# Strassen FFN in a two-layer decoder: order of weight loads, row sums and shared additions

## The chip, the cores and the metric
The kernel is one program on 1 core of a Trainium2 chip. The metric is the device time of one execution in microseconds (us); the median of 3 runs before the change is 2208.37 us (2204.72 to 2210.13). The engines are named as the profile names them: PE (TensorE, matmuls), DVE (VectorE), ACT (ScalarE), POOL (GpSimd) and SP (SyncE, which issues DMAs here).

## The reference
Two layers, each a token mixer and then a gated MLP with a causal convolution of width 3, on x of 1024 x 1024 in float32. The change touches the MLP alone (and, by two lines, the start of layer 1's mixer):

```python
def conv_ffn(x, norm_g, w_up, conv_w, conv_b, w_down):
    h = causal_depthwise_conv(rms_norm(x, norm_g) @ w_up, conv_w, conv_b)
    g, u = jnp.split(h, 2, axis=-1)
    return (jax.nn.silu(g) * u) @ w_down

for layer in range(DEPTH):
    x = x + (pool_diffattn_layer if layer % 2 == 0 else mlstm_layer)(x, ...)
    x = x + conv_ffn(x, ...)
```

w_up is 1024 x 5632, w_down 2816 x 1024. The hidden width is cut in FC = 22 rows of 128 channels.

## The kernel before
Each float32 matrix is cut into a high and a low part, and a product is three matmuls (high x high, high x low, low x high) of 128 x 128 weights with 512 columns.

**Up stage.** Block j (0 to 21) makes row j of g and of u at once, as one 2 x 2 Strassen-Winograd product: seven half-size products of 12 matmuls each, on PE in the order a11, s2, s3, s1, a22, a12, s4. Their weights come from two raw tiles (a g tile and a u tile, loaded by SP into a ring of 3): POOL makes the sums s1 to s4 (`pool_s1` to `pool_s4`), ACT copies each of the seven to its high part (`act_cut`, a "cut"), POOL subtracts to get the low part (`pool_low`, a "low"). The ring holds 6 of these weights, so a cut waits until PE has finished the product 6 places earlier. DVE adds the products up: u2, u3, then c22, c21 (hg, the g row) and c11, c12 (hu, the u row), multiplies both by the norm factor (`dve_hg`, `dve_hu`), and after ACT's centre tap (`act_center`, into PSUM) adds the two other taps. ACT's silu and DVE's `dve_gated` give the gated row in one of two buffers; SP stores it in `gated_rows`. PE's a22 of block j waits for u3 of block j; u2 and u3 stand on DVE behind the taps of hu of block j-1.

ACT's own order in block j is: cut a12(j), silu(j-1), the copy p1(j), cut s4(j), centre of hu(j-1), then cuts a11, s2, s3, s1, a22 of block j+1 and the centre of hg(j). Everything on an engine runs in program order.

**T sums.** Rows 4 to 19 are taken in pairs into a second Strassen product in the down stage. When both rows of a pair are stored, four sums of halves are made in place (`dve_pair_t`, on DVE in the even blocks 6 to 20) and stored by SP (`sp_pair_out`). The buffers are needed again by `dve_gated` two rows later.

**Down stage.** Rows 20, 0, 1, 2 are multiplied plainly (4 rows, `pe_down`), then come 8 Strassen blocks m = 0 to 7 (`pe_block`), then rows 3 and 21. In a Strassen block the order on PE is again a11, s2, s3, s1, a22, a12, s4, and the weights are made as above. Each block m also has to bring in the pair inputs for block m+2: ACT issues the loads (`act_pair_load`), cuts them in two parts (`act_pair_split`, half 0 and half 1), DVE makes the low parts (`dve_pair_low_half`). The sums on DVE are u1, u2 (a shared U), e22, c22, e21, a11, c12. U is shared: only in the last two blocks (m = 6, 7) is it added to three output quarters, v22, v21, v12. In block 6 DVE also makes the low parts of rows 3 and 21 (`dve_gated_low`), which wait for ACT's cuts of those rows (`act_gated_high`), and these stand on ACT behind the cut s3 of block 7. PE's a11 of block 7 waits for DVE's a11 addition of block 6, its a22 for e22, its s4 for c22.

**Start of layer 1.** The first three weight tiles of the mixer are cut by POOL (`pool_cut`); POOL also adds the squares of the norm (`add_squares`).

Of the kernel before, what the change touches and what calls it, by code (L numbers as in the profile page):

```python
# [10 lines left out]
ALU = mybir.AluOpType  # L11
# [18 lines left out]
DOWN_ORDER = (FC - 2, 0, 1, 2, 3, FC - 1)  # L30
# [53 lines left out]
def program(nc, x_in, pos_in, wall, pool_w, params, lam4, consts, scratch, gated_rows, out):  # L84
    with ExitStack() as ctx:
# [1448 lines left out]
        def block_parts(m):  # L1534

            shared = ("v22", "v21", "v12") if m >= N_BLOCK - 2 else ()
            return ("u1",) * (m >= 2) + ("u2",) + shared + ("e22", "c22", "e21", "a11", "c12")
# [392 lines left out]
        def dve_pair_t(dve, f, r):  # L1930

            b11, b12, b21, b22 = (f.ab[:, i, h * HALF:(h + 1) * HALF] for i in range(2) for h in range(2))
            at0 = f.l * SUMS + 3 * (KC // 2) + 4 * r
            dve.wait_ge(a_out, 16 * (f.l * A_OUT + out_at(PAIR0 + 2 * r + 1)))
            dve.tensor_tensor(b22, b22, b12, ALU.subtract).then_inc(tt_made, 1)
            dve.wait_ge(tt_made, at0 + 1)
            dve.tensor_tensor(b12, b12, b11, ALU.subtract).then_inc(tt_made, 1)
            dve.wait_ge(tt_made, at0 + 2)
            dve.tensor_tensor(b11, b11, b22, ALU.add).then_inc(tt_made, 1)
            dve.wait_ge(tt_made, at0 + 3)  # L1940
            dve.tensor_tensor(b21, b21, b11, ALU.subtract).then_inc(tt_made, 1)

# [9 lines left out]
        def dve_block_add(dve, f, m, name, to, room):  # L1952

            dve.tensor_tensor(to, room.rearrange("p (a s) -> p a s", a=2), to, ALU.add).then_inc(parts, 1)  # L1954

# [8 lines left out]
        def dve_block(dve, f, m):  # L1964
# [14 lines left out]
            if m >= N_BLOCK - 2:  # L1979
                dve_block_done(dve, f, m, "u2")  # L1980
                for row, half in ((1, 1), (1, 0), (0, 1)):
                    to = f.res_of(m, row, half)
                    dve.tensor_tensor(to, u, to, ALU.add).then_inc(parts, 1)  # L1983
                dve_block_done(dve, f, m, "v12")
            dve_block_prod(dve, f, m, "s3")
            dve_block_add(dve, f, m, "e22", f.res_of(m, 1, 1), f.block_room("s3"))
            dve_block_prod(dve, f, m, "s1")
            dve_block_done(dve, f, m, "e22")
            dve_block_add(dve, f, m, "c22", f.res_of(m, 1, 1), f.block_room("s1"))
            if m + 2 < N_PAIR:  # L1990
# [11 lines left out]
            dve_block_prod(dve, f, m, "s4")  # L2002
            dve_block_add(dve, f, m, "c12", f.res_of(m, 0, 1), f.block_room("s4"))
# [115 lines left out]
        def dve_ffn(dve, l):  # L2119
# [15 lines left out]
            for j in range(1, FC - 1):  # L2135
# [9 lines left out]
                if j >= PAIR0 + 2 and j % 2 == 0:  # L2145
                    dve_pair_t(dve, f, (j - PAIR0 - 2) // 2)
# [6 lines left out]
            dve_gated(dve, f, j - 1)  # L2153
# [3 lines left out]
            dve_c11(dve, f, j)  # L2157
            dve_gated_low(dve, f, 1)
            dve_c12(dve, f, j)
# [15 lines left out]
        def act_ffn(act, l):  # L2175
# [51 lines left out]
            for m in range(N_BLOCK):  # L2227
                q = m + 2
                for i in range(N_PROD):
# [12 lines left out]
                    if i == 4 and q < N_PAIR:  # L2242
                        act_pair_split(act, f, q, 1)
# [55 lines left out]

        def sp_gated_out(sp, f, j):  # L2300
# [17 lines left out]
        def sp_ffn(sp, l):  # L2318
            f = Ffn_of[l]
            for j in range(FC):  # L2320
                if j >= 3:
                    sp_gated_out(sp, f, j - 3)
                sp_load(sp, f.T0 + 2 * j)
                if j - 3 > PAIR0 and j % 2 == 0:
                    sp_pair_out(sp, f, (j - 3 - PAIR0) // 2)
                sp_load(sp, f.T0 + 2 * j + 1)
# [10 lines left out]
        def pool_ffn(pool, l):  # L2337
# [15 lines left out]
            for j in range(1, N_UP):  # L2353
# [10 lines left out]
                pool_low(pool, f, j, "a22")  # L2364
                pool_low(pool, f, j, "a12")
# [1005 lines left out]
```

## Time and profile before

| | |
|---|---|
| median of 3 runs | 2208.37 us (2204.72 to 2210.13) |
| profiled execution, its own time | 2209.51 us |
| span in the profile | 2207.7 us |
| PE busy | 2128.8 us, 96% |
| DVE, ACT, POOL busy | 1428.8, 890.0, 1257.0 us |
| up stage from block 7 to its end, each layer | 316.21 and 315.93 us |
| Strassen blocks of the down stage, each layer | 164.04 and 164.50 us |

The execution's own time is 1.8 us more than its span (what lies before the first and behind the last instruction). The profile gives for every instruction its start, its length, the idle time of its engine ahead of it and what ended that idle time. PE is nearly always busy, so what matters is where it stands still and what it then waits for.

### The profile page before, as it was taken

How to read it: one execution, taken by the hardware profiler on the slowest of the kernel's cores; microseconds unless marked ns; L12 is line 12 of the kernel's file. 1: busy time of each engine (PE TensorE's matmuls, PEld its weight loads, DVE VectorE, ACT ScalarE, POOL GpSimd, SP SyncE). 2: the span in 40 equal slices, each digit the busy share in tenths (PEclk: the TensorE clock that was granted, in tenths of full speed). 3: DMA queues.
4: the chain of work that ended last, by engine and by line, in shares of the span. 5: the costliest groups of instructions: out<-in, count | busy, mean ns of one | idle time of the engine just before them, and what ended most of it. 6: DMA issues, size and time to landing. Idle time of an engine off the chain costs nothing. (4 is left out here: it accounts for less than half of the span.)

```text
span 2207.7 us, 26911 instructions
## 1 busy us (share of the span) xinstructions
PE 2128.8 (96%) x10027; PEld 1747.9 (79%) x10027; DVE 1428.8 (65%) x1545; ACT 890.0 (40%) x1396; POOL 1257.0 (57%) x808
## 2 busy tenths in 40 slices
PE   9999999999999999998999999999999999999988
PEld 8777778778777777887788898888787777778877
DVE  7776767677767767566744244286777777675665
ACT  6555452543343343333334433434443333343331
POOL 2212217777677674688553333267876776655883
PEclk9999999999999999999999999999999999999999
DMA  6111012022322324333321021030223222333432
GB/s 205 54 48 49 25 50 103 29 86 77 124 86 96 113 97 173 123 129 109 129 87 51 27 77 58 20 134 29 87 86 104 97 98 100 108 129 139 152 125 86
DMA packets 57345, 204.19 MB, mean 92 GB/s; under 512 B 6848, under 2 KB 8960, under 8 KB 55168
## 3 DMA queue, kind: packets, MB, share of 16 engines
q1 hardware_dynamic: 47136, 163.22, 22.1%
q10 hardware_dynamic: 10080, 39.24, 4.8%
q8 instruction: 81, 1.33, 0.2%
q14 instruction: 48, 0.39, 0.1%
HBM read 151.81 MB, written 46.43 MB: 90 GB/s over the span
## 5 line engine op out<-in xcount | busy, mean ns | idle before, releaser
L1695 POOL TENSOR_TENSOR w_lo<-w_sum,w_hi 128x512 fp32r<-128x512 f32 x240 | 362.0, 1517 | 211.0 <-ACT w_hi L1689 211.0
L2296 POOL TENSOR_TENSOR w_hi<-w_raw,ones 128x1024 fp32r<-128x1024 f32 x54 | 106.3, 1969 | 491.6 <-PE pj L336 170.4
L1689 ACT ACTIVATE w_hi<-w_sum 128x512 fp32r<-128x512 f32 x240 | 146.3, 627 | 492.3 <-POOL w_sum L1710 223.3
L1695 POOL TENSOR_TENSOR w_lo<-w_raw,w_hi 128x512 fp32r<-128x512 f32 x180 | 236.5, 1321 | 107.4 <-ACT w_hi L1689 107.4
L1764 PE MATMUL pj<-t_hi,w_hi 128*128 128x512 f32 x520 | 210.5, 405 | 46.6 <-DVE ffn_v L1873 46.6
L1764 PE MATMUL pj<-t_lo,w_hi 128*128 128x512 f32 x520 | 207.9, 400 | 0.0
L1764 PE MATMUL pj<-t_hi,w_lo 128*128 128x512 f32 x520 | 207.7, 399 | 0.0
L1839 PE MATMUL dn<-pair,w_hi 128*128 128x512 f32 x512 | 159.1, 392 | 8.4 <-DVE res L1954 8.4
L1689 ACT ACTIVATE w_hi<-w_raw 128x512 fp32r<-128x512 f32 x180 | 111.4, 625 | 138.3 <-PE pj L1764 59.5
L1764 PEld LDWEIGHTS pj<-t_hi,w_hi 128*128 128x128 f32 x520 | 100.0, 192 | 78.4 <-issue 58.4
L2298 POOL TENSOR_TENSOR w_lo<-w_raw,w_hi 128x1024 fp32r<-128x1024 f32 x54 | 135.9, 2516 | 4.2
L1764 PE MATMUL pj<-xa_hi,w_hi 128*128 128x512 f32 x348 | 136.2, 391 | 1.6 <-DVE xa_lo L1458 0.9
L1764 PE MATMUL pj<-xb_hi,w_hi 128*128 128x512 f32 x348 | 135.8, 390 | 1.5 <-DVE xb_lo L1458 0.9
L1764 PE MATMUL pj<-xa_lo,w_hi 128*128 128x512 f32 x348 | 135.8, 390 | 0.0
L1764 PE MATMUL pj<-xb_lo,w_hi 128*128 128x512 f32 x348 | 135.6, 390 | 0.0
L1764 PE MATMUL pj<-xa_hi,w_lo 128*128 128x512 f32 x348 | 135.4, 389 | 0.0
L1764 PE MATMUL pj<-xb_hi,w_lo 128*128 128x512 f32 x348 | 135.4, 389 | 0.0
L1839 PE MATMUL pj<-pair,w_hi 128*128 128x512 f32 x384 | 120.1, 394 | 9.4 <-DVE pair L1950 7.7
L363 PE MATMUL pj<-xb_hi,w_hi 128*128 128x512 f32 x384 | 128.2, 415 | 0.0
L1839 PEld LDWEIGHTS dn<-pair,w_hi 128*128 128x128 f32 x512 | 96.8, 190 | 30.1 <-issue 10.0
L363 PE MATMUL pj<-xb_lo,w_hi 128*128 128x512 f32 x384 | 119.2, 392 | 0.0
L363 PE MATMUL pj<-xb_hi,w_lo 128*128 128x512 f32 x384 | 118.5, 390 | 0.0
(421 smaller groups left out, 5460.6 us busy)
## 6 DMA issues: line engine op xcount, KB each, us to landing
w_raw<-weights SPq DMA_DIRECT2D x187, 512.0 KB, 4.1
gated_rows<-ffn_gated SPq DMA_DIRECT2D x72, 512.0 KB, 2.9
pair_stage<-gated_rows ACTq DMA_DIRECT2D x16, 1024.0 KB, 6.4
pair_stage<-gated_rows ACTq DMA_DIRECT2D x16, 512.0 KB, 4.5
x_first<-x_t SPq DMA_DIRECT2D x8, 512.0 KB, 7.7
res<-x_t SPq DMA_DIRECT2D x8, 512.0 KB, 6.5
pair_stage<-gated_rows ACTq DMA_DIRECT2D x16, 256.0 KB, 3.5
scratch<-res ACTq DMA_DIRECT2D x8, 512.0 KB, 2.6
```

Source lines behind the costliest of these rows:

```text
L363: ins = pe.matmul(o[:, t * HALF:(t + 1) * HALF], w, x[:, k, t * HALF:(t + 1) * HALF], start=(first and m == 0), stop=(last and m == 2))
L1689: act.activation(f.cut(t, whi), f.source(j, name), ACT.Copy).then_inc(c_high, 1)
L1695: pool.tensor_tensor(f.cut(t, wlo), f.source(j, name), f.cut(t, whi).bitcast(F32), ALU.subtract).then_inc(c_ready, 1)
L1764: ins = pe.matmul(o, f.cut(t, w)[:, k * P:(k + 1) * P], f.moving(name, x, k), start=(not more and k == 0 and q == 0), stop=(k == KC // 2 - ...
L1839: ins = pe.matmul(room[:, d * HALF:(d + 1) * HALF], f.cut(t, w)[:, at0:at0 + P], f.pair_block(2 * c + q, x, name), start=(not more and q = ...
L2296: pool.tensor_tensor(whi[:, w, :], raw[:, r, :], ones[:, 0:1].to_broadcast([P, D]), ALU.mult).then_inc(w_high, 1)
L2298: pool.tensor_tensor(wlo[:, w, :], raw[:, r, :], whi[:, w, :].bitcast(F32), ALU.subtract).then_inc(w_ready, 1)
```

## The change
Seven edits, none of which changes what PE multiplies or in what order:

1. SP: in block j of the up stage the load of the first weight tile stands ahead of the store of gated row j-3, and the load of the second ahead of the stores of the T sums.
2. The four T sums go from DVE (even blocks 6 to 20) to POOL (odd blocks 7 to 21, between the low of a22 and the low of a12).
3. ACT: both halves of a pair are cut directly behind each other, behind the cut a11 of the next block; the second half stood behind the cuts s2 and s3.
4. DVE, blocks 6 and 7: the shared additions v22, v21, v12, which stood together ahead of e22, are spread: v22 behind e22, v21 behind c22, v12 behind e21.
5. The plain rows come in the order 0, 20, 1, 2, with row 0 read back from memory.
6. DVE, last block of the up stage: the gated row 20 is made behind c11, and the first low stands alone ahead of it.
7. POOL, start of layer 1: the first weight tile is cut ahead of the squares 1 to 3, the second ahead of the squares 4 and 5.

```diff
-DOWN_ORDER = (FC - 2, 0, 1, 2, 3, FC - 1)
+DOWN_ORDER = (0, FC - 2, 1, 2, 3, FC - 1)
...
+        def dve_block_share(dve, f, m, row, half):
+            to = f.res_of(m, row, half)
+            dve.tensor_tensor(to, f.u[m % 2][:, :, :], to, ALU.add).then_inc(parts, 1)
...
             dve_block_add(dve, f, m, "u2", u, f.block_room("s2"))
-            if m >= N_BLOCK - 2:
-                dve_block_done(dve, f, m, "u2")
-                for row, half in ((1, 1), (1, 0), (0, 1)):
-                    to = f.res_of(m, row, half)
-                    dve.tensor_tensor(to, u, to, ALU.add).then_inc(parts, 1)
-                dve_block_done(dve, f, m, "v12")
             dve_block_prod(dve, f, m, "s3")
             dve_block_add(dve, f, m, "e22", f.res_of(m, 1, 1), f.block_room("s3"))
+            dve_block_done(dve, f, m, "e22")
+            if m >= N_BLOCK - 2:
+                dve_block_share(dve, f, m, 1, 1)
+                dve_block_done(dve, f, m, "v22")
             dve_block_prod(dve, f, m, "s1")
-            dve_block_done(dve, f, m, "e22")
             dve_block_add(dve, f, m, "c22", f.res_of(m, 1, 1), f.block_room("s1"))
+            if m >= N_BLOCK - 2:
+                dve_block_share(dve, f, m, 1, 0)
...
             dve_block_add(dve, f, m, "e21", f.res_of(m, 1, 0), f.block_room("a22"))
+            if m >= N_BLOCK - 2:
+                dve_block_share(dve, f, m, 0, 1)
             dve_block_prod(dve, f, m, "a12")
             dve_block_add(dve, f, m, "a11", f.res_of(m, 0, 0), f.block_room("a12"))
...
                 dve_taps(dve, f, j, 0)
-                if j >= PAIR0 + 2 and j % 2 == 0:
-                    dve_pair_t(dve, f, (j - PAIR0 - 2) // 2)
                 dve_c12(dve, f, j)
...
             j = FC - 1
             dve_u2(dve, f, j)
             dve_u3(dve, f, j)
-            dve_gated(dve, f, j - 1)
             dve_c22(dve, f, j)
             dve_c21(dve, f, j)
             dve_gated_low(dve, f, 0)
             dve_c11(dve, f, j)
+            dve_gated(dve, f, j - 1)
+            dve_c12(dve, f, j)
             dve_gated_low(dve, f, 1)
-            dve_c12(dve, f, j)
...
                     if i == 2 and q < N_PAIR:
                         act_pair_split(act, f, q, 0)
-                    if i == 4 and q < N_PAIR:
                         act_pair_split(act, f, q, 1)
...
             for j in range(FC):
+                sp_load(sp, f.T0 + 2 * j)
                 if j >= 3:
                     sp_gated_out(sp, f, j - 3)
-                sp_load(sp, f.T0 + 2 * j)
+                sp_load(sp, f.T0 + 2 * j + 1)
                 if j - 3 > PAIR0 and j % 2 == 0:
                     sp_pair_out(sp, f, (j - 3 - PAIR0) // 2)
-                sp_load(sp, f.T0 + 2 * j + 1)
...
                 pool_low(pool, f, j, "a22")
+                if PAIR0 + 2 < j < FC and j % 2 == 1:
+                    pool_pair_t(pool, f, (j - PAIR0 - 3) // 2)
                 pool_low(pool, f, j, "a12")
...
             for n in range(T_MIX1, T_FFN1):
-                if n == T_MIX1:
+                if n == T_MIX1 + 1:
                     for c in range(1, 4):
                         add_squares(pool, 2, c)
-                if n == T_MIX1 + 1:
+                if n == T_MIX1 + 2:
                     for c in (4, 5):
```

`pool_pair_t` holds the four subtractions and additions of `dve_pair_t` word for word, each waiting for the one before it, on `pool` in place of `dve`.

POOL, one odd block of the up stage, as it stands in the changed kernel (w_sum_118 is s1 and later s4, w_sum_119 is s2, w_sum_120 is s3, ffn_gated the two gated rows):

```order
L1696 TENSOR_TENSOR w_lo<-w_sum_118,w_hi 128x512
L1696 TENSOR_TENSOR w_lo<-w_raw,w_hi 128x512
L2300 TENSOR_TENSOR ffn_gated_134<-ffn_gated_134 128x512
L2302 TENSOR_TENSOR ffn_gated_134<-ffn_gated_134 128x512
L2304 TENSOR_TENSOR ffn_gated_134<-ffn_gated_134 128x512
L2306 TENSOR_TENSOR ffn_gated_134<-ffn_gated_134 128x512
L1696 TENSOR_TENSOR w_lo<-w_raw,w_hi 128x512
L1723 TENSOR_TENSOR w_sum_118<-w_raw,w_sum_119 128x512
```

Before, the same place on POOL read:

```order
L1717 TENSOR_TENSOR w_sum_120<-w_raw 128x512
L1695 TENSOR_TENSOR w_lo<-w_sum_120,w_hi 128x512
L1695 TENSOR_TENSOR w_lo<-w_sum_118,w_hi 128x512
L1695 TENSOR_TENSOR w_lo<-w_raw,w_hi 128x512 x2
L1722 TENSOR_TENSOR w_sum_118<-w_raw,w_sum_119 128x512
```

The four T sums now stand between the low of a22 and that of a12, and so ahead of the sum s4 of the same block.

DVE, block m = 6 of the down stage, before (down_u is U; res<-dn or pj are e22, c22, e21, a11 and c12; L1983 are the shared additions; act_last the lows of rows 3 and 21):

```order
L1983 TENSOR_TENSOR res<-down_u_0_153,res 128x2x512 x3
L1954 TENSOR_TENSOR res<-dn,res 128x2x512 x2
L2007 TENSOR_TENSOR act_last_1_138<-act_stage_141,act_last_0_137 128x1024
L1954 TENSOR_TENSOR res<-dn,res 128x2x512
L1954 TENSOR_TENSOR res<-pj,res 128x2x512
L2007 TENSOR_TENSOR act_last_3_140<-ffn_gated_134,act_last_2_139 128x1024
```

and of the change:

```order
L1942 TENSOR_TENSOR res<-dn,res 128x2x512
L1947 TENSOR_TENSOR res<-down_u_0_153,res 128x2x512
L1942 TENSOR_TENSOR res<-dn,res 128x2x512
L1947 TENSOR_TENSOR res<-down_u_0_153,res 128x2x512
L2005 TENSOR_TENSOR act_last_1_138<-act_stage_141,act_last_0_137 128x1024
L1942 TENSOR_TENSOR res<-dn,res 128x2x512
L1947 TENSOR_TENSOR res<-down_u_0_153,res 128x2x512
L1942 TENSOR_TENSOR res<-pj,res 128x2x512
L2005 TENSOR_TENSOR act_last_3_140<-ffn_gated_134,act_last_2_139 128x1024
```

One of the three shared additions now stands between the low of row 3 and the a11 addition (res<-pj); e22 stands ahead of all of them.

ACT, block m = 5 of the change (pair_0_146 is the high part of the last pair, w_sum_119, 120 and 118 the cuts s2, s3 and s1 of block 6):

```order
L2059 DMA pair_stage_0_142<-gated_rows 128x2048
L1690 ACTIVATE w_hi<-w_raw 128x512
L2080 ACTIVATE pair_0_146<-pair_stage_0_142 128x1536
L2080 ACTIVATE pair_0_146<-pair_stage_0_142 128x2048
L1690 ACTIVATE w_hi<-w_sum_119 128x512
L1690 ACTIVATE w_hi<-w_sum_120 128x512
L1690 ACTIVATE w_hi<-w_sum_118 128x512
```

The second half (128x2048) stood between w_sum_120 and w_sum_118; it now follows the issue of its own load by two instructions.

## Rows read from the trace of the kernel before

**Rows 1.** Who PE waited for, whole span: us in total, times, longest us
```profile
PE pj L1764 <- DVE ffn_v L1873: 46.6, 30, 2.3
PE dn L1839 <- DVE res L1954: 8.4, 4, 4.0
PE pj L1839 <- DVE pair L1950: 7.7, 4, 3.1
PE pj L2565 <- issue: 4.2, 1, 4.2
```

**Rows 2.** The same for the up stage from block 7, layer 0 and layer 1
```profile
PE pj L1764 <- DVE ffn_v L1873: 20.9, 13, 2.3
...
PE pj L1764 <- DVE ffn_v L1873: 20.7, 13, 2.0
```

**Rows 3.** Windows, block 4 and blocks 7 to 21: us, engines' busy (x), PEclk, DMA
```profile
489.77:508.81 19.04, 19.04 (x85) 15.77 (x84) 13.99 (x14) 8.14 (x11) 15.02 (x12) 1.00 0.25 83
546.89:863.10 316.21, 295.30 (x1260) 239.95 (x1259) 223.96 (x228) 120.67 (x165) 216.26 (x160) 0.98 0.31 107
```

**Rows 4.** Timeline of PE, first matmul of a22, blocks 15 and 16: start, us, [idle before]
```profile
728.12 0.47 PE L1764 MATMUL pj<-t_hi,w_hi 128*128 128x512 f32 x1 [1.96 <-DVE ffn_v L1873]
...
748.49 0.47 PE L1764 MATMUL pj<-t_hi,w_hi 128*128 128x512 f32 x1 [1.08 <-DVE ffn_v L1873]
```

**Rows 5.** Timeline of ACT: hu centres in blocks 15 and 16, cut s4 of 16
```profile
722.74 1.20 ACT L2022 ACTIVATE dn<-ffn_hu,params 128x1024 f32<-128x1024 f32 x1
...
742.58 0.63 ACT L1689 ACTIVATE w_hi<-w_sum 128x512 fp32r<-128x512 f32 x1 [0.15 <-POOL w_sum L1722]
743.12 1.19 ACT L2022 ACTIVATE dn<-ffn_hu,params 128x1024 f32<-128x1024 f32 x1
```

**Rows 6.** Timeline of DVE, block 15: the hu multiply
```profile
721.67 0.69 DVE L1912 TENSOR_TENSOR ffn_hu<-ffn_hu,rms_bc 128x512 f32<-128x512 f32 x1
```

**Rows 7.** Timeline of POOL: low a22 and sum s4 of 15, sums s1, s2 of 17
```profile
714.20 1.28 POOL L1695 TENSOR_TENSOR w_lo<-w_raw,w_hi 128x512 fp32r<-128x512 f32 x1
...
717.29 1.74 POOL L1722 TENSOR_TENSOR w_sum<-w_raw,w_sum 128x512 f32<-128x512 f32 x1
...
746.20 1.28 POOL L1703 TENSOR_TENSOR w_sum<-w_raw 128x512 f32<-128x512 f32 x1
747.62 1.27 POOL L1710 TENSOR_TENSOR w_sum<-w_sum,w_raw 128x512 f32<-128x512 f32 x1
```

**Rows 8.** Timeline of SP's queue: the load behind the stores of the T sums
```profile
721.49 0.47 SPq L2284 DMA_DIRECT2D w_raw<-weights  x1
```

**Rows 9.** Timeline of DVE, block m = 6, layer 0: shared additions, low of row 3, a11
```profile
1032.59 6.75 DVE L1983 TENSOR_TENSOR res<-down_u,res 128x1024 f32<-128x1024 f32 x3
...
1046.91 1.47 DVE L2007 TENSOR_TENSOR act_last<-act_stage,act_last 128x1024 fp32r<-128x1024 f32 x1 [4.99 <-ACT act_last L2041]
...
1049.44 1.21 DVE L1954 TENSOR_TENSOR res<-pj,res 128x1024 f32<-128x1024 f32 x1
```

**Rows 10.** Timeline of ACT, block m = 6: cut s3 of block 7
```profile
1045.30 0.63 ACT L1689 ACTIVATE w_hi<-w_sum 128x512 fp32r<-128x512 f32 x1 [2.70 <-POOL w_sum L1717]
```

**Rows 11.** Timeline of PE, m = 7: first matmuls, a22; first matmuls in layer 1
```profile
1050.75 0.70 PE L1839 MATMUL pj<-pair,w_hi 128*128 128x512 f32 x2
...
1062.66 0.70 PE L1839 MATMUL dn<-pair,w_hi 128*128 128x512 f32 x2 [0.76 <-DVE res L1954]
...
2162.39 0.70 PE L1839 MATMUL pj<-pair,w_hi 128*128 128x512 f32 x2 [1.61 <-issue]
```

**Rows 12.** Timeline of ACT, block m = 2: load of half 1, cut s2 of block 3
```profile
952.22 0.33 ACTq L2061 DMA_DIRECT2D pair_stage<-gated_rows  x1
...
958.17 0.63 ACT L1689 ACTIVATE w_hi<-w_sum 128x512 fp32r<-128x512 f32 x1 [2.94 <-POOL w_sum L1710]
```

**Rows 13.** The page, DMA issues: median us to landing
```profile
pair_stage<-gated_rows ACTq DMA_DIRECT2D x16, 1024.0 KB, 6.4
```

**Rows 14.** Timeline of DVE, start of layer 1: last plain addition of the down stage
```profile
1100.23 1.21 DVE L2113 TENSOR_TENSOR res<-dn,res 128x1024 f32<-128x1024 f32 x1
```

More of the change, by code:

```diff
@@ L1534, in block_parts @@
         def block_parts(m):
-            shared = ("v22", "v21", "v12") if m >= N_BLOCK - 2 else ()
-            return ("u1",) * (m >= 2) + ("u2",) + shared + ("e22", "c22", "e21", "a11", "c12")
+            if m >= N_BLOCK - 2:
+                return ("u1", "u2", "e22", "v22", "c22", "v21", "e21", "v12", "a11", "c12")
+            return ("u1",) * (m >= 2) + ("u2", "e22", "c22", "e21", "a11", "c12")
         def block_part(m, name):
@@ L1928, in dve_gated @@
             dve.tensor_tensor(f.a[j % 2], f.sg[:, :], f.y[1], ALU.mult).then_inc(gated, 1)
[L1930 to L1941, printed above, removed]
         PIECE = ((0, 3 * HALF), (3 * HALF, 7 * HALF))
@@ L1994, in dve_block @@
             dve_block_prod(dve, f, m, "a22")
+            if m >= N_BLOCK - 2:
+                dve_block_done(dve, f, m, "v21")
             dve_block_add(dve, f, m, "e21", f.res_of(m, 1, 0), f.block_room("a22"))
+            if m >= N_BLOCK - 2:
+                dve_block_share(dve, f, m, 0, 1)
             dve_block_prod(dve, f, m, "a12")
@@ L2002, in dve_block @@
             dve_block_prod(dve, f, m, "s4")
+            if m >= N_BLOCK - 2:
+                dve_block_done(dve, f, m, "v12")
             dve_block_add(dve, f, m, "c12", f.res_of(m, 0, 1), f.block_room("s4"))
@@ L2298, in pool_cut_free, with pool_pair_t @@
             pool.tensor_tensor(wlo[:, w, :], raw[:, r, :], whi[:, w, :].bitcast(F32), ALU.subtract).then_inc(w_ready, 1)
+        def pool_pair_t(pool, f, r):
+            b11, b12, b21, b22 = (f.ab[:, i, h * HALF:(h + 1) * HALF] for i in range(2) for h in range(2))
+            at0 = f.l * SUMS + 3 * (KC // 2) + 4 * r
+            pool.wait_ge(a_out, 16 * (f.l * A_OUT + out_at(PAIR0 + 2 * r + 1)))
+            pool.tensor_tensor(b22, b22, b12, ALU.subtract).then_inc(tt_made, 1)
+            pool.wait_ge(tt_made, at0 + 1)
+            pool.tensor_tensor(b12, b12, b11, ALU.subtract).then_inc(tt_made, 1)
+            pool.wait_ge(tt_made, at0 + 2)
+            pool.tensor_tensor(b11, b11, b22, ALU.add).then_inc(tt_made, 1)
+            pool.wait_ge(tt_made, at0 + 3)
+            pool.tensor_tensor(b21, b21, b11, ALU.subtract).then_inc(tt_made, 1)
         def sp_gated_out(sp, f, j):
```

## The prediction
> **What bounds the kernel now.** I read who PE waited for first [rows 1]. PE stands still for some 68 us in all, in three places that the change touches: 30 stops in the up stages, where a22 waits for DVE's u3 (46.6 us), 8 stops in the Strassen blocks of the down stages (8.4 and 7.7 us, and the 1.6 of rows 11), and one of 4.2 us where layer 1 begins. The rest of the 2209.51 us is PE at work, and the change leaves that work as it is. So the question is only which stops go, and which come instead.
>
> From block 7 on, each up stage has 13 such stops, 20.9 and 20.7 us [rows 2]. A block without a stop takes 19.04 us [rows 3], 15 of them 285.6; the stage took 316.21. Beyond the stops 9.7 us are left: restarts, and stretches at the lower of PE's two clock levels (the mean granted clock is 0.98 there and 1.00 in the quiet block).
>
> Why a22 stops is read from two neighbours [rows 4, 5]. In block 15 ACT's centre of hu starts at 722.74 and PE's a22 at 728.12, 5.38 later; in block 16 they are 743.12 and 748.49, 5.37 apart. Between lie the centre, two taps, u2 and u3. So a22 starts 5.4 us behind the hu centre, and every us by which that centre is late is a us of stop. In the odd block it is late because DVE's hu multiply (721.67) stands behind the four T sums [rows 6]. In the even block it is late because the cut s4, ahead of it on ACT, waited for POOL's sum s4 [rows 5]: POOL ran late since SP's load at 721.49 stood behind the stores of the T sums [rows 8].
>
> In the down stage I asked what block 7 waits for. PE starts it at 1050.75 [rows 11], 0.10 after DVE's a11 addition of block 6 ends (1049.44 + 1.21) [rows 9]. That addition follows the low of row 3 at 1046.91, for which DVE had sat idle 4.99 us until ACT's cut of row 3; that cut stands directly behind the cut s3, which waited for POOL's sum s3 until 1045.30 [rows 10]. POOL makes these sums without waiting for PE. So the start of block 7 hangs on POOL's own pace, and the stops ahead of it (up to 4.0 and 3.1 us, rows 1) cost nothing: PE would only have arrived earlier. In layer 1 it stopped a further 1.61 us there [rows 11].
>
> **The change part by part.**
>
> *Loads ahead of stores, and no T sums on DVE.* The even stops go: 5 in each layer. In each layer 8 odd stops remain to be judged.
>
> *T sums on POOL in the odd blocks.* They stand between the low of a22 and that of a12, so ahead of sum s4, cut s4 and the hu centre. In block 15 the low of a22 ended at 714.20 + 1.28 = 715.5; without the even stop ahead of it and with the load in time, POOL is up to 0.9 earlier, held then only by the ring: 714.6 to 715.5. T sums wait for each other; the price of such a step is the distance from s1 to the s2 that waits for it, 747.62 - 746.20 = 1.42, and the last takes 1.27 [rows 7]: 3 x 1.42 + 1.27 = 5.5 us. DVE's hu multiply falls into them; a POOL sum beside a DVE operation with both inputs in SBUF took 1.74 instead of 1.28 [rows 7], so + 0.45. Then the low of a12 1.27, sum s4 1.28, cut s4 and its release 0.6 [from rows 5: 743.12 - 742.58]. Sum 9.1: the centre starts at 723.7 to 724.6, where it started at 722.74. The stop grows from 1.96 to 2.9, or at worst to 3.8. I take 2.9, since the even stops, which made POOL late, are gone. 8 x 2.9 = 23.2 against 20.9: + 2.3 a layer, + 4.6 in all. Bounds: T sums as quick as DVE's multiply of the same size (0.69, rows 6) would put the centre near 720.5 and leave next to no stop, - 41.6; the worst end is 8 x 3.8, + 19.
>
> On the Trainium skill, "SBUF — State Buffer", section "Who interferes with whom": of GpSimd and a VectorE operation with two SBUF inputs, the one issued second is blocked until the first has finished. The row agrees in kind, not in size (0.46 lost beside a 0.69 us multiply); by the rule in full the 16 odd stops would be 0.24 longer each, + 4 us.
>
> *The clock.* The 9.7 us a layer beyond the stops come with 8 stops of about 2 us; the stops become 2.9 and fewer are short. Between no change and growth with the stop's length (9.7 x 2.9 / 1.96 = 14.4, + 4.7) I take the middle, + 2.4 a layer, + 4.8.
>
> *Both halves cut together.* The stops for the pair's low part (7.7 us in four, rows 1) go, but they lie ahead of block 7's start. On ACT the second half now waits for its own load: issued at 952.22 [rows 12], such a load lands about 6.4 us later [rows 13], and the split of 2048 columns takes some 2 (the centre of 1024 takes 1.2, rows 5), so the cut s2 of block 3 comes near 960.5 instead of 958.17 [rows 12]: 2 us later for POOL, of which some comes back where the split no longer stands ahead of the cut s1. In the later blocks, where POOL's s2 is later itself, it is a wash. Over five blocks POOL ends 0 to 1.5 us later; I take + 1 a layer, bounds - 3 and + 5.
>
> *Shared additions spread.* e22 is done at once, so the stop of 4.0 us ahead of a22 goes, again ahead of block 7's start. On the path that sets that start one of the three additions now lies between the low of row 3 and the a11 addition: three took 6.75 us beside a busy POOL [rows 9], 2.25 each; less what it no longer costs POOL earlier (0.4 to 0.6), + 1.7. In block 7 the stop ahead of a22 (0.76, rows 11, and its restart) goes: - 0.9. With the splits + 1.8 a layer, + 3.6 in all.
>
> PE now reaches block 7's start some 10 to 12 us early and stands there in one piece. After the 4.2 us stop of rows 1 PE came back at the lower clock level; after this one I take 2 us of lost work a layer, + 4 in all, bounds 0 and + 7.
>
> *Row order and the last block.* The first two plain rows change places. DVE makes one low (1.2) later, and silu and the last gated row come about 0.8 later on a path with 1.5 to spare: 0, at worst + 1 a layer.
>
> *Start of layer 1.* The cut no longer waits for the squares, so the 4.2 us stop shrinks. What is late next is the last plain addition, which DVE ends at 1100.23 + 1.21 = 1101.44 [rows 14] and without which PE can't use its fourth PSUM room: it would work from 1092.7 for 5 us and then stand until 1101.4. Bounds 0 and - 6.9; I take - 2.5.
>
> **Sum.** 4.6 + 4.8 + 3.6 + 4 - 2.5 = + 14.5 on the profiled 2209.5; that execution was 1.1 above the median, so 2208.4 + 14.5 = 2222.9. The largest terms have their better bounds nearer than their worse ones (the clock terms above all), so I round to 2220.
>
> **The rivals.**
>
> A. *The stops just go.* If POOL gets through the T sums before they matter and block 7 doesn't hang on POOL, the 41.6 us of rows 2, the 17 of the down stage and some clock are saved: about 2150. Half of it (the up stage alone) gives 2175. For it: POOL is busy only 216 of 316 us in the stage [rows 3]. Against it: its spare time lies elsewhere than ahead of sum s4. A milder form: POOL is further ahead, so that the T sums begin 1.5 us earlier than I say; the odd stop is then 1.4, the up stages save 19 and more of clock, about 2195. The ring speaks against it: the cut of a22 waits for a product of the block before. Together 0.14.
>
> B. *No change.* The odd stop is 2.9 but the clock terms are nil (- 8.8) and the start of layer 1 gives its full 6.9: 2208.4 + 4.6 + 3.6 - 6.9, 2209.7. 0.26.
>
> C. *POOL becomes the bound of the whole up stage.* A pair of blocks asks POOL for 22 weight operations at 1.28 and 4 T sums at 1.4, with ACT's cuts between them; the pair took 41.5 (20.4 from the one a22 to the next in rows 4, and 19.04 + 2.1 where the odd stop lies) and would take 43. 16 x 1.5 = + 24, with the down stage and layer 1 (3.6 + 4 - 2.5) + 29: 2237. Speaks for it: every sum that POOL lowers goes through ACT and back, and POOL waits. Against: the ring is 6 deep, and in block 4 it lets POOL rest 4 of 19 us [rows 3]. 0.10.
>
> **How the numbers follow.** My forecast, slower by a longer odd stop and a late block 7, has 0.50. A measurement of this kernel tells about 0.3% (6.6 us) from no change. Faster by more than that (below 2201.8): rival A whole and a little of B, 0.16. Within it (to 2215.0): most of B and the low end of the forecast, 0.28. Slower: 0.56. The range of 8 in 10 goes from 2198, which takes in the mild form of A, to 2236, where the worse bounds of the odd stop lie; the forecast's own range is 2211 to 2232.
>
> **What would show it.** In the profile after: PE's waits for u3 number 8 a layer from block 7 on, all in odd blocks, each near 2.9 us; ahead of each, ACT's cut s4 waits for POOL's sum s4, and the centre follows it. No stop in even blocks. In block m = 6 no stop ahead of a22, none for a pair's low part, but one stop of about 10 us at the first matmul of block 7, for DVE's a11 addition, with ACT's cut of row 3 behind POOL's sum s3 as before. At layer 1 a short stop after some 42 matmuls. The forecast is wrong if the odd stops are shorter than 2 us, or if block 7 starts right behind block 6.

## The result, and the profile after

The changed kernel takes 2250.3 us (median of three runs, 2241.9 to 2250.9) against 2208.37: ratio 1.018, 95% interval 1.014 to 1.022. It is slower, as I had forecast, but by 42 us instead of 12, and outside the range that I gave. The profiled run took 2241.9 us (span 2240.1); it is the shortest of the three, with a mean granted clock of 0.976 where the other two have 0.973 and 0.972. So the profile shows 32.4 of the 42 us; the rest is taken up in the part on the prediction.

The waits of PE over the whole span of the changed kernel (engine, line, who ended the wait: us in total, times, longest), which answer to [rows 1]:
```profile
PE pj L1765 <- DVE ffn_v L1874: 59.0, 20, 3.4
PE pj L1840 <- POOL w_lo L1696: 17.6, 4, 8.3
PE dn L2575 <- DVE res L2111: 3.7, 1, 3.7
```
The waits for u3 are fewer (20 instead of 30) and longer (59.0 instead of 46.6 us in all). In the down stage the stops of rows 1 have become one of 8.3 us a layer, ahead of block 7, and a few of under 0.5 us; that of layer 1's start went from 4.2 to 3.7 us. The up stage from block 7 on in windows, first layer and second (us, then busy time of PE, PEld, DVE, ACT and POOL, PE's granted clock, DMA share, GB/s), which answer to [rows 3]:
```profile
545.34:875.28 329.94, 302.93 (x1261) 246.96 (x1260) 199.77 (x195) 121.91 (x163) 258.40 (x192) 0.94 0.29 102
1672.95:2005.07 332.12, 305.11 (x1262) 248.54 (x1261) 201.06 (x195) 121.88 (x163) 256.55 (x192) 0.93 0.29 102
```
Counted in the same way, up to the first matmul of the down stage, they took 316.4 and 316.2 us before (the window of rows 3 ends 0.24 us earlier), at 0.98. Here lie 29.4 of the 32.4 us between the two profiled runs.

The timeline of one odd block, 13, in the changed kernel (start, duration, engine, line, operation, output <- inputs, idle time before and who ended it), which answers to [rows 4 to 7]:
```profile
672.53 1.28 POOL L1696 TENSOR_TENSOR w_lo<-w_raw,w_hi 128x512 fp32r<-128x512 f32 x1
673.77 1.29 POOL L2300 TENSOR_TENSOR ffn_gated<-ffn_gated 128x512 f32<-128x512 f32 x1
...
676.07 0.91 DVE L1913 TENSOR_TENSOR ffn_hu<-ffn_hu,rms_bc 128x512 f32<-128x512 f32 x1
...
676.51 1.61 POOL L2304 TENSOR_TENSOR ffn_gated<-ffn_gated 128x512 f32<-128x512 f32 x1
...
678.21 1.29 POOL L2306 TENSOR_TENSOR ffn_gated<-ffn_gated 128x512 f32<-128x512 f32 x1
679.45 1.29 POOL L1696 TENSOR_TENSOR w_lo<-w_raw,w_hi 128x512 fp32r<-128x512 f32 x1
680.70 1.30 POOL L1723 TENSOR_TENSOR w_sum<-w_raw,w_sum 128x512 f32<-128x512 f32 x1
...
682.09 0.64 ACT L1690 ACTIVATE w_hi<-w_sum 128x512 fp32r<-128x512 f32 x1 [4.99 <-POOL w_sum L1723]
682.63 1.19 ACT L2020 ACTIVATE dn<-ffn_hu,params 128x1024 f32<-128x1024 f32 x1
...
687.16 0.69 DVE L1874 TENSOR_TENSOR ffn_v<-pj,ffn_v 128x512 f32<-128x512 f32 x1
```
```profile
688.00 0.47 PE L1765 MATMUL pj<-t_hi,w_hi 128*128 128x512 f32 x1 [3.37 <-DVE ffn_v L1874]
```
DVE has the hu multiply done at 676.98, but ACT's centre starts only at 682.63: it stands behind the cut s4, which waited 4.99 us for POOL's sum s4, and that sum stands behind the four T sums. a22 follows the centre by 5.37 us, as before. So the mechanism is the one in the prediction; the stop is 3.38 us instead of 2.9.

What the prediction had far too small is what comes behind the stop. PE in block 15 of the same run, after the same stop:
```profile
731.35 0.77 PE L1765 MATMUL pj<-t_hi,w_hi 128*128 128x512 f32 x1 [3.38 <-DVE ffn_v L1874]
731.91 0.63 PE L1765 MATMUL pj<-t_lo,w_hi 128*128 128x512 f32 x1
...
736.17 0.63 PE L1765 MATMUL pj<-t_hi,w_lo 128*128 128x512 f32 x1
736.60 0.52 PE L1765 MATMUL pj<-xb_hi,w_hi 128*128 128x512 f32 x1
...
739.47 0.39 PE L1765 MATMUL pj<-xb_hi,w_hi 128*128 128x512 f32 x1
739.70 0.39 PE L1765 MATMUL pj<-xb_lo,w_hi 128*128 128x512 f32 x1
```
The twelve matmuls of a22 start 0.43 us apart (1.2 GHz) and take 5.25 us; at 0.227 us apart (2.4 GHz, the last two rows) they take 2.72. That one stop costs 3.4 us of standing and 2.5 us of slow work. It is one of the dearer: in the first layer seven of the eight stops have matmuls at 1.2 GHz behind them, those of blocks 7, 9 and 13 for a shorter time, and that of block 11 has none.

The start of block 7 of the down stage, which answers to [rows 9 to 11]:
```profile
1054.95 1.26 POOL L1718 TENSOR_TENSOR w_sum<-w_raw 128x512 f32<-128x512 f32 x1
1056.31 0.63 ACT L1690 ACTIVATE w_hi<-w_sum 128x512 fp32r<-128x512 f32 x1 [2.67 <-POOL w_sum L1718]
1056.84 1.04 ACT L2039 ACTIVATE act_last<-act_stage 128x1024 fp32r<-128x1024 f32 x1
...
1057.91 1.45 DVE L2005 TENSOR_TENSOR act_last<-act_stage,act_last 128x1024 fp32r<-128x1024 f32 x1 [7.58 <-ACT act_last L2039]
...
1061.70 1.21 DVE L1942 TENSOR_TENSOR res<-pj,res 128x1024 f32<-128x1024 f32 x1
```
```profile
1063.01 1.19 PE L1840 MATMUL pj<-pair,w_hi 128*128 128x512 f32 x2 [8.32 <-POOL w_lo L1696]
```
The chain is as forecast: sum s3 on POOL, cut s3, cut of row 3, low of row 3, the e21 and the shared addition, a11 addition (done at 1062.91), PE 0.10 later. The wait is put down to POOL here, but the addition is what came last. Block 7 itself, in a window:
```profile
1063.01:1085.40 22.39, 21.65 (x84) 17.39 (x85) 16.02 (x12) 2.76 (x3) 10.45 (x6) 0.89 0.31 95
```
The granted clock is 0.89 in it; it took 20.15 us before.

At the start of layer 1, which answers to the 4.2 us of [rows 1]:
```profile
1116.14 0.59 PE L2575 MATMUL dn<-w_hi,xb_hi 128*128 128x264 f32 x1 [3.67 <-DVE res L2111]
```
PE no longer waits for the first cut, but, some 42 matmuls on, for the last plain addition of DVE.

### The profile page after: what moved, and what is told of

Same layout as the page of the kernel before. It is cut to its first block and busy times, and to the rows that moved or that the text cites. A ratio compares the mean times of both kernels' runs of the same rounds, so it can differ in the third digit from the quotient of the medians.

```text
span 2240.1 us, 26915 instructions
## 1 busy us (share of the span) xinstructions
PE 2146.7 (96%) x10027; PEld 1762.8 (79%) x10027; DVE 1385.3 (62%) x1481; ACT 897.4 (40%) x1396; POOL 1336.5 (60%) x872
## 5 line engine op out<-in xcount | busy, mean ns | idle before, releaser
L1765 PE MATMUL pj<-t_hi,w_hi 128*128 128x512 f32 x520 | 217.6, 418 | 59.0 <-DVE ffn_v L1874 59.0
L1765 PE MATMUL pj<-t_lo,w_hi 128*128 128x512 f32 x520 | 215.0, 413 | 0.0
L1765 PE MATMUL pj<-t_hi,w_lo 128*128 128x512 f32 x520 | 215.0, 413 | 0.0
L1765 PEld LDWEIGHTS pj<-t_hi,w_hi 128*128 128x128 f32 x520 | 104.5, 201 | 88.6 <-issue 66.9
L1919 DVE SCALAR_TENSOR_TENSOR dn<-ffn_hu,params,dn 128x1022 f32<-128x1022 f32 x44 | 56.6, 1286 | 145.8 <-ACT dn L2020 145.8
L1765 PE MATMUL pj<-xb_hi,w_lo 128*128 128x512 f32 x348 | 135.4, 389 | 0.0
L1765 PE MATMUL pj<-xb_lo,w_hi 128*128 128x512 f32 x348 | 135.4, 389 | 0.0
L1765 PEld LDWEIGHTS pj<-t_hi,w_lo 128*128 128x128 f32 x520 | 105.1, 202 | 23.3
L1765 PEld LDWEIGHTS pj<-t_lo,w_hi 128*128 128x128 f32 x520 | 105.2, 202 | 21.7
```

What stands on the lines that cost most here:

```text
L1765: ins = pe.matmul(o, f.cut(t, w)[:, k * P:(k + 1) * P], f.moving(name, x, k), start=(not more and k == 0 and q == 0), stop=(k == KC // 2 - ...
L1919: dve.scalar_tensor_tensor(y[:, 2:S], h[:, 0:S - 2], f.tap(j, m, 0), y[:, 2:S], ALU.mult, ALU.add).then_inc(taps, 1)
```

## The experiments

Each ratio is to the kernel before, on the same chip. "The stage" is the up stage from block 7 on.

**T sums back on DVE.** `pool_pair_t` and its call are taken out, and in `dve_ffn` stands again
```
                 dve_taps(dve, f, j, 0)
+                if j >= PAIR0 + 2 and j % 2 == 0:
+                    dve_pair_t(dve, f, (j - PAIR0 - 2) // 2)
                 dve_c12(dve, f, j)
```


> The changed kernel with the T sums back on DVE in the even blocks; loads ahead of stores and all the rest stay. Theory 1 (the up stage is set by how late ACT's hu centre is, and the clock costs more than the stops themselves): the even stops stay away, since the load is in time, and the odd stop goes back from 3.38 to about 1.96 us; 8 of them, 15.7 a layer, with some 5 us of lower clock: up stage from block 7 on at 306 to 311 us instead of 330 and 332, total 2250.3 - 2 x 21 = 2208. Theory 2 (it was the load order that hurt, or the down stage): the up stages stay above 325 us and the total above 2240.

Measured: ratio 0.9972 (0.9962 to 0.9982), 2199 us; stages of 310.2 and 309.8 us, 8 stops each, 16.0 and 15.7 us in all. Theory 1 holds. This edit alone is worth 1.0181 - 0.9972, 2.1% of the time, and makes the change slower. Ahead of the stop in block 13 (the first and the third row are T sums on DVE, the second is POOL's sum s4):
```profile
673.62 0.99 DVE L1936 TENSOR_TENSOR ffn_gated<-ffn_gated 128x512 f32<-128x512 f32 x1
...
674.02 1.74 POOL L1723 TENSOR_TENSOR w_sum<-w_raw,w_sum 128x512 f32<-128x512 f32 x1
674.65 1.67 DVE L1938 TENSOR_TENSOR ffn_gated<-ffn_gated 128x512 f32<-128x512 f32 x1
```
A T sum takes 0.69 us on DVE where nothing of POOL runs beside it, but 1.67 where it was issued while POOL's sum ran. The Trainium skill, "SBUF — State Buffer", section "Who interferes with whom", says that of two such operations the one issued second is blocked until the first is done; by that, as an estimate, it would end 0.69 us after POOL's 675.76, at 676.45, and it ended at 676.32. So here the trace agrees with the rule in size too.

The prediction had read the row of 1.74 us in [rows 7] as a sum beside a 0.69 us multiply. It was not: the hu multiply starts at 721.67, and what ran on DVE when that sum was issued, at 717.29, was a T sum, in the kernel before:
```profile
716.88 0.99 DVE L1935 TENSOR_TENSOR ffn_gated<-ffn_gated 128x512 f32<-128x512 f32 x1
```
Of it 0.58 us were left, and POOL's sum lost 0.46, so that row is close to the rule as well.

**The hu centre ahead of the cut s4.**
```
+                    if i == 1 and j > 1:
+                        act_center(act, f, j - 1, 1)
                     if t < N_PROD * FC:
                         act_cut(act, f, t)
...
-                    if i == 1 and j > 1:
-                        act_center(act, f, j - 1, 1)
```


> The changed kernel with one pair of instructions exchanged on ACT: the centre of hu stands ahead of the cut s4 instead of behind it; T sums stay on POOL, whole. Theory 1 (the odd stop is the centre standing behind a cut that waits for POOL's late sum s4): all 16 stops for u3 go or fall under 0.5 us, the up stages take 286 to 291 us from block 7 on and the total is 2250.3 - 2 x 42 = 2166 (2160 to 2180). Theory 2 (POOL itself is too slow in the odd blocks): the stop only moves, PE now waits for POOL's low of s4 or of the next block's first tiles, 3 us as before, and the total stays within 2240 to 2255.

Measured: ratio 0.9938 (0.9923 to 0.9953), 2191 us; stages of 304.2 and 303.6 us. All odd stops are gone, and 7 even ones of 1.17 and 2.18 us stand in each stage. So what set the odd stop was indeed the place of the centre behind that cut. But neither theory had the even ones, and the time is 25 us above the 2166 of theory 1.

**Both centres ahead.** As before, and the centre of hg likewise ahead of `act_cut` at `i == 6`.

> The changed kernel with both centres moved up on ACT: hu's ahead of the cut s4 (as in the run before with that alone, which left stops of 1.17 and 2.18 us in the even blocks), and hg's ahead of the cut s1 of the next block. Theory 1 (the remaining even stops come from the hg centre, which stood behind cuts that waited for POOL, late by the T sums): they fall under 0.8 us, up stages near 290 instead of 304, ratio 0.9938 - 2 x 14 / 2208 = 0.981. Theory 2 (they come from DVE multiplies that are slower beside POOL's sums: 1.53 and 2.26 us instead of 0.69 and 1.23): the stops stay above 1 us, ratio 0.990 or more.

Measured: ratio 0.9881 (0.9865 to 0.9896); stages of 300.9 and 300.3 us, 4 even stops of 1.0 to 2.65 us in each. The numbers of theory 1 missed, and stops above 1 us are what theory 2 said, but the rows of block 14 bear out the cause of theory 1 and not that of theory 2 (the hu multiply takes 0.80 us at 689.68):
```profile
684.16 1.15 ACT L1690 ACTIVATE w_hi<-w_sum 128x512 fp32r<-128x512 f32 x2 [2.70 <-POOL w_sum L1718]
...
685.21 1.19 ACT L2020 ACTIVATE dn<-ffn_hg,params 128x1024 f32<-128x1024 f32 x1
...
686.44 1.29 DVE L1919 SCALAR_TENSOR_TENSOR dn<-ffn_hg,params,dn 128x1022 f32<-128x1022 f32 x1 [6.02 <-ACT dn L2020]
```
```profile
695.90 0.47 PE L1765 MATMUL pj<-t_hi,w_hi 128*128 128x512 f32 x1 [2.61 <-DVE ffn_v L1874]
```
The hg centre still stands behind two cuts, the first of which waited 2.70 us for POOL's sum s3; DVE stood idle 6.02 us for it. So with the T sums on POOL moving one centre is not enough: a cut that waits for a late sum holds up whatever is behind it on ACT.

**T sums on half, three quarters and seven eighths of their columns.**
```
-            b11, b12, b21, b22 = (f.ab[:, i, h * HALF:(h + 1) * HALF] for i in range(2) for h in range(2))
+            b11, b12, b21, b22 = (f.ab[:, i, h * HALF:h * HALF + HALF // 2] for i in range(2) for h in range(2))
```
(`HALF * 3 // 4` and `HALF * 7 // 8` in the others.) These kernels leave out the rest of the T sums; they serve to make the stop shorter in steps, with everything else in its place.

> The changed kernel with each of POOL's T sums on half of its columns (the other halves of T1 and T2 are not made). The four sums should take 3 instead of 5.7 us and the odd stop 3.38 - 2.7 = 0.7 us. Theory 1 (clock): the stretches at 1.2 GHz in the up stages go nearly all with it, so the up stages fall from 330 and 332 to about 292, total 2250.3 - 2 x 38 = 2174. Theory 2 (only the stops count, the clock is an accident of this execution): the total falls by 16 x 2.7 = 43 us, to 2207.

> The changed kernel with POOL's T sums on three quarters of their columns (the rest of T1 and T2 isn't made). Half gave stops of 1.22 us and no stretch at 1.2 GHz in the up stages, whole ones 3.38 us and stretches of 3.41 and 6.83 us: these should give stops of 2.3 us. Theory 1 (each stop of 2 us or more is followed by one stretch of 3.41 us at the lower clock, in which about 1.4 us of work is lost): the up stage from block 7 on takes 285.6 + 8 x (2.3 + 0.4 + 1.4) = 318, total against the half sums + 2 x 21, ratio 0.9867 + 0.0186 = 1.005. Theory 2 (the lower clock comes only with the 3.4 us stops): 307 us a stage, ratio 0.995.

> The changed kernel with POOL's T sums on seven eighths of their columns (the rest of T1 and T2 isn't made). By the runs with half, three quarters and all of them (1.22, 2.27, 3.38 us) the stop will be 2.8 us, about the 2.9 of my forecast, so this run shows what the clock does at the stop that I forecast. Theory 1 (the loss at the lower clock grows evenly from 2.1 us a stage at 2.27 to 14 at 3.38): 8 us, stage 285 + 8 x 3.2 + 8 = 319, 20 us above the run with three quarters, ratio 1.006. Theory 2 (it is a step that lies above the stop I forecast): stage 313, ratio 1.001 or less. Theory 3 (the step lies between 2.3 and 2.8): stage 325, ratio 1.012 or more.

Measured: ratios 0.9867 (0.9852 to 0.9882), 0.9972 (0.9961 to 0.9983) and 1.0077 (1.0060 to 1.0094). The stage of the first layer, in the order half, three quarters, seven eighths:
```profile
547.01:844.50 297.49, 287.71 (x1261) 235.91 (x1260) 193.70 (x195) 121.19 (x163) 240.09 (x192) 1.00 0.32 114
```
```profile
545.38:854.32 308.94, 290.90 (x1261) 238.18 (x1260) 200.32 (x195) 121.43 (x163) 249.66 (x192) 0.99 0.31 109
```
```profile
546.88:866.62 319.74, 296.76 (x1261) 242.42 (x1260) 195.47 (x195) 121.55 (x163) 255.86 (x192) 0.97 0.30 106
```
What the stage costs beyond its stops is its length less 15 quiet blocks (285.6) less the stops; "at 1.2 GHz" is how long the granted clock stood at the lower level. Mean of both layers, us:
```
                        stops each   stops   stage   beyond   at 1.2 GHz   granted clock
T sums in pieces, DVE        -         0.3   288.4     2.5        0            1.00
half                       1.22        9.8   297.5     2.1        0            1.00
T sums on DVE              1.96       15.9   310.0     8.5       13.7          0.98
three quarters             2.27       18.0   308.9     5.3        6.8          0.99
seven eighths              2.87       23.0   319.1    10.5       18.8          0.97
changed kernel             3.38       27.0   331.0    18.4       41.0          0.94, 0.93
T sums on POOL only        3.38       27.0   336.3    23.7       54.6          0.92
```
Stops of 1.22 us cost their length only. From 2.27 to 3.38 us the part beyond the stops grows more than threefold while the stops grow by half, and the time at 1.2 GHz grows with it.

The rows are of one profiled run each, and at equal stops runs of one kernel differ in their clock: those of the changed kernel took 2241.9 (0.976) to 2250.9 (0.972), those with the T sums on POOL only 2242.1 (0.976) to 2251.6 (0.970). The profiles are of the 2241.9 and of the 2251.6, so the 5 us a stage between the last two lines say nothing of the kernels. In the same way the profile with the T sums on DVE is of the longest of nine runs (2202.6), that with three quarters of the shortest of ten (2197.4), while the ratios of the two kernels are the same, 0.9972. If what parts a profiled run from the median of its kernel lies in the two stages (an estimate), the part beyond is 6.9, 6.9, 11.4, 22.6 and 21.5 us in the last five lines: it does not fall from 1.96 to 2.27, and it rises most steeply above 2.87.

With half the columns theory 1 is near (297.5, 292 expected; the stop was 1.22 instead of 0.7). With three quarters the stage is near theory 2 (307 expected, 318 by theory 1), though not all the lower clock is gone. Seven eighths gives the stop of my forecast, and lies near theory 1 (319, ratio 1.006).

**The down stage as before** (splits apart, the three shared additions behind u2).

> The changed kernel with the down stage as it was: the pair's splits apart, the three shared U additions behind u2, in blocks 6 and 7. By the profile of the changed kernel the last two blocks cost 2.8 and 2.7 us more than before and blocks 0 to 5 0.2 and 0.9 less, so theory 1 says 2250.3 - 4.4 = 2246. My forecast's terms for this part (3.6 and 4) said 2250.3 - 7.6 = 2242.7. Rival: the single long stop ahead of block 7 also costs clock behind it in runs that were not profiled, and 10 us or more come back, 2240 or less.

Measured: ratio 1.0164 (1.0149 to 1.0179). Against 1.0181 that is 3.8 us less, by ratios whose intervals overlap; the profiles have the two down stages 4.1 us shorter. Theory 1 (4.4) fits, but the timing alone doesn't show it, nor does it part it from the 7.6 of my terms. In the profile blocks 6 and 7 are back at 28.8 and 20.2 us (28.9 and 22.4 in the changed kernel), and the separate stops are there again (7.6 us for the pairs' low parts).

**Row 3 loaded and cut earlier in block 6.**
```
-                    if i == 1 and q == N_PAIR:
+                    if i == 0 and q == N_PAIR:
                         act.wait_ge(act_lo, f.l * AC + pair_at(N_PAIR, 0))
                         gated_in(act, f, STAGES - 1)
...
-                    if i == 4 and q == N_PAIR:
+                    if i == 2 and q == N_PAIR:
                         for p in range(DOWN_SIZES[0], len(DOWN_ORDER)):
                             act_gated_high(act, f, p)
```


> The changed kernel with the load of gated row 3 issued ahead of the cut s4 on ACT and the cuts of the last two rows ahead of block 7's cuts s2 and s3, all in block 6 of the down stage. Theory 1 (block 7 stands because ACT's cut of the row is behind a cut that waits for POOL): DVE's low of the row comes at once, the a11 addition of block 6 keeps PE's pace, the 8.3 us stop ahead of block 7 and the 10 us at 1.2 GHz behind it go; block 6 takes 20.3 us instead of 28.9 and block 7 20.2 instead of 22.4, so 2 x 11 = 22 us less, ratio to before 1.0181 - 0.0100 = 1.008. Theory 2 (POOL's lows of block 7, which the profile names as what ended the stop, are the bound): the stop shrinks to no less than 5 us, since POOL makes the low of a12 of block 7 only at about 1061, and the ratio stays at 1.014 or above.

Measured: ratio 1.0096 (1.0081 to 1.0111), 19 us less than the changed kernel.
```profile
1051.10 1.04 ACT L2039 ACTIVATE act_last<-act_stage 128x1024 fp32r<-128x1024 f32 x1
...
1053.94 2.31 DVE L2005 TENSOR_TENSOR act_last<-act_stage,act_last 128x1024 fp32r<-128x1024 f32 x1
...
1058.44 1.21 DVE L1942 TENSOR_TENSOR res<-pj,res 128x1024 f32<-128x1024 f32 x1
```
```profile
1059.75 0.71 PE L1840 MATMUL pj<-pair,w_hi 128*128 128x512 f32 x2 [1.37 <-POOL w_lo L1696]
```
The low no longer waits, the stop ahead of block 7 is 1.37 instead of 8.32 us, and the two blocks take 21.7 and 20.1 us in the first layer, 22.9 and 20.1 in the second. PE starts block 7 0.10 us after the a11 addition again (1058.44 + 1.21). POOL's lows were not the bound: theory 1.

**Loads ahead of stores alone**, on the kernel before (the edit of the change in `sp_ffn`, nothing else).

> The kernel before with one edit of the change alone: SP's loads ahead of the stores of the same block. Theory 1 (the even stops are made by the late load of g): the even stops go, 8 odd ones of 1.96 stay, the up stages from block 7 on take 310 instead of 316.3 us, and the rest is as before: - 12.5 us, ratio 0.994. Theory 2 (the even stops go only if the T sums' place on DVE or the stores move too): 13 stops stay, ratio 0.999 to 1.001.

Measured: ratio 0.9951 (0.9937 to 0.9966), 2196 us; stages of 308.6 and 309.9 us with 8 stops (16.0 and 15.7 us). Theory 1: the late load made the even stops.

**T sums on POOL alone**, on the kernel before (with the last block's order, no other edit).

> The kernel before with the T sums on POOL and the last block's order alone (no loads ahead of stores, down stage and start of layer 1 as before). Theory 1 (late load and late centre add up): odd stops of 3.4 us and even ones of about 1, up stages from block 7 on 335 to 342 us, ratio to before 1.0181 + 0.005 + 0.001 = 1.022 to 1.026. Theory 2 (the load no longer comes late, since POOL, not SP, is behind): stages as in the changed kernel, 330 to 332, ratio 1.015 to 1.018.

Measured: ratio 1.0184 (1.0162 to 1.0206).
```profile
547.32:883.72 336.40, 309.42 (x1261) 251.61 (x1260) 197.82 (x195) 122.44 (x163) 260.14 (x192) 0.92 0.29 100
```
Of each theory one half holds. There are 8 stops of 3.38 us and no even ones, though the load stands behind the stores, and the ratio is about that of the changed kernel (theory 2). The stage is 336 us, as theory 1 had it, but by the clock of this run, not by more stops. With the T sums on POOL the order of loads no longer matters for the stops.

**T sums on DVE in two pieces**, where DVE waits for ACT's centres (the last argument: 0 makes b22 and b12, 1 makes b11 and b21).
```
                 dve_c11(dve, f, j)
+                if j >= PAIR0 + 2 and j % 2 == 0:
+                    dve_pair_t(dve, f, (j - PAIR0 - 2) // 2, 0)
                 dve_taps(dve, f, j, 0)
                 dve_c12(dve, f, j)
                 dve_hu(dve, f, j)
+                if j >= PAIR0 + 2 and j % 2 == 0:
+                    dve_pair_t(dve, f, (j - PAIR0 - 2) // 2, 1)
                 dve_taps(dve, f, j, 1)
```


> The changed kernel with the T sums back on DVE, but in two pieces where DVE waits for ACT anyway: two ahead of the taps of hg, two between the hu multiply and the taps of hu (with all four between those taps and c12, as in the run of T sums on DVE, the odd stop was 1.96 us and the up stages from block 7 on took 310.2 and 309.8). Theory 1 (the stop is the lateness of the hu centre, nothing else): the hu multiply comes 2 to 2.8 us earlier, all 8 stops a layer fall under 0.8 us or go, no stretches at the lower clock remain in the stage, and it takes 286 to 292 us: ratio to before 0.9972 - 2 x 20 / 2208 = 0.979. Theory 2 (DVE itself has no spare time in such a pair of blocks): the stop stays at 1.5 us or more, wherever the sums stand, and the ratio at 0.99 or above.

Measured: ratio 0.9785 (0.9763 to 0.9806), 2159 us.
```profile
545.58:833.98 288.40, 287.71 (x1262) 235.87 (x1260) 223.92 (x226) 118.66 (x162) 221.01 (x160) 1.00 0.34 117
```
```profile
665.44 0.69 DVE L1913 TENSOR_TENSOR ffn_hu<-ffn_hu,rms_bc 128x512 f32<-128x512 f32 x1
666.05 0.68 DVE L1942 TENSOR_TENSOR ffn_gated<-ffn_gated 128x512 f32<-128x512 f32 x1
...
666.76 1.21 ACT L2035 ACTIVATE dn<-ffn_hu,params 128x1024 f32<-128x1024 f32 x1
666.76 0.69 DVE L1944 TENSOR_TENSOR ffn_gated<-ffn_gated 128x512 f32<-128x512 f32 x1
```
One stop of 0.4 us is left in 15 blocks. Theory 1: the sums cost next to nothing beside the centres for which DVE had to wait. The same four sums cost 22 us a stage more in one place on DVE (310.0 - 288.4), 43 more on POOL (331.0 - 288.4).

**Both repairs together** (T sums in two pieces on DVE, row 3 earlier; the edits are those of the two runs above).

> The changed kernel with both repairs: T sums on DVE in two pieces, and gated row 3 loaded and the last rows cut earlier in block 6. Theory 1 (they are in different stages and add up): 0.9785 and a further (1.0181 - 1.0096) = 0.0085 off, ratio to before 0.970, 2139 us. Rival (the long stop ahead of block 7 only paid for lateness that comes out elsewhere, since PE now comes to the down stage without stops behind it): half of it, ratio 0.974.

Measured: ratio 0.9713 (0.9698 to 0.9727), 2143.6 us, granted clock 0.997 over the whole run. Stages 288.5 and 288.2 us, block 6 of the down stage 21.9 and 21.8. The gains add up (0.970 expected; the rival's 0.974 lies outside the interval), and this version beats both kernels: 63 us under the kernel before, 103 under the changed one, by the ratios.

## Why the prediction was right in its mechanism and wrong in its size

The profiled runs differ by 32.4 us, where the terms gave 14.5. The stops are 7.8 us more than forecast and the clock 12.2; the down stage is 3.2 less, and the start of layer 1 gives back 0.9 less.

- *The odd stop* was forecast at 2.9 us (bounds to 3.8) and is 3.38. The chain itself was priced right: from the end of the low of a22 to the centre 8.82 us (682.63 - 673.81) against 9.1. In it the third T sum, beside the hu multiply, took 0.32 us more than the others (1.61), where I had 0.45. What was wrong is where it starts. I took POOL 0.9 us earlier than before, since the even stops were to go; the low of a22 ends 10.8 us ahead of the point at which PE would start a22, where it was 10.7 [rows 4, 7], so 0.14 earlier. 0.76 later and 0.28 shorter: 0.48. Up to two lows ahead of that of a22 POOL was indeed 0.8 us earlier (they begin 15.6 us ahead of that point, 684.63 - 669.03, where it was 14.8, 726.16 - 711.39). But they took 3.53 us instead of 2.85, beside DVE's hg multiply, which itself took 2.33 instead of 1.23: that is 0.68 of the 0.76, and the term for it was missing.
```profile
669.03 3.53 POOL L1696 TENSOR_TENSOR w_lo<-w_sum,w_hi 128x512 fp32r<-128x512 f32 x2 [0.81 <-ACT w_hi L1690]
669.07 2.33 DVE L1893 TENSOR_TENSOR ffn_hg<-ffn_hg,rms_bc 128x1024 f32<-128x1024 f32 x1
```
```profile
711.39 2.85 POOL L1695 TENSOR_TENSOR w_lo<-w_sum,w_hi 128x512 fp32r<-128x512 f32 x2 [0.80 <-ACT w_hi L1689]
```
In sum the stops cost + 12.4 us (2 x 27.0 against 41.6) instead of + 4.6.
- *The clock*, the step that failed. I had + 4.8 us for both layers, the middle between nothing and growth in proportion to the stop; what each stage costs beyond its stops went from 9.9 us (to the same end point) to 18.4, + 17.0 in both. Two errors lie in it. The growth is steeper than the length of the stop (the table above), so the upper end of the bound, proportion (+ 9.4), was no upper end. And I let the term stand at its middle when I took the worst stop for the range: the 2236 holds stops of up to 3.8 us, but not the clock that goes with them. The run with seven eighths separates the two: at a stop of 2.87 us, the one I had forecast, the ratio is 1.0077, 2225 us, inside my range, and the term was large enough (2 x (10.5 - 9.9) = 1.2 in the profiles). The last half us of each stop cost the other 23 us; in the profiles 16 x 0.51 = 8.2 of standing and 2 x (18.4 - 10.5) = 15.8 of clock.
- *From the profiles to the medians* it is a further 9.5 us (42 against 32.4). The median run of the changed kernel is 8.4 us above the profiled one, at a granted clock of 0.973 instead of 0.976; as an estimate, the part of the span below full clock, 0.027 x 2248.5 against 0.024 x 2240.1, is 7 us longer. So the clock term at the median is nearer + 26 than + 17.
- *No even stops*: right. The reason given, the load in time, holds where the T sums are on DVE; with them on POOL the even stops go without it.
- *Block 7 of the down stage*: right in every link, the stop 8.3 us where I had about 10. The price was + 7.6 us (3.6 and 4 of clock) and is + 4.4. I had block 7 start 2.7 us later in each layer; it starts 0.3 us later in the first and 0.6 earlier in the second, counted from the stage's begin. In the long stop's wake PE works at 1.2 GHz, as taken, and block 7 is 2.2 and 2.5 us longer where I had 1.1.
- *Start of layer 1*: a stop of 3.67 us, for the last plain addition, as named. - 1.6 instead of - 2.5 us.
- *Row order*: 0, as taken.

Of the rivals, A (the stops just go) is borne out nowhere in the changed kernel. B needed the clock terms to be nil, and they were the largest. C's 2237 was nearer than my 2220 for another reason than its own: POOL does not bound the even blocks, which have no stop at all.

Open: why the cost of a stop rises so steeply above 2.87 us, and why at equal stops of 3.38 us PE spent 37.5 and 44.4 us of the two stages at the lower level in one profiled run and 54.6 us of each in another. The runs show the granted clock there, not its cause.

## What to carry to other kernels

Before an operation is moved to an idler engine, look at what stands behind it in that engine's queue and in the queue of whoever waits for it: POOL had 100 us to spare in the stage, DVE 92, but only DVE's lay beside the centre. A wait for another engine in the middle of a queue is the place to put such work. And count a stop of PE by its length and by the matmuls behind it: with stops of 1.96 us and more those were at half speed in part, with 1.22 they were not, and at 3.38 us that added 60 to 80% of the stop's own length (16 to 22 us a stage to 27.0).

## What the runs showed of the hardware that I had not expected

- The cost of a stop is far from proportional to its length: eight stops a stage of 1.22 us left the granted clock at 1.00, of 2.87 at 0.97, of 3.38 at 0.92 to 0.94.
- At equal stops runs of one kernel differ in their clock: 2241.9 to 2250.9 us at 0.976 to 0.972 in the changed kernel.
- A DVE addition issued while POOL's ran took 1.67 instead of 0.69 us, while POOL's took 1.74 instead of 1.29: each paid where it came second.
